# Attention heads of the second block in pairs on halves of the TensorE array, in place of one head after another

## The reference, cut to what matters

```
mixer_a: for three groups (window, dilation) = (128, 1), (512, 4), (2048, 16):
           q, k, v of 16 heads each, rotary embedding on q and k,
           causal banded attention with that dilation
         the groups are merged by their softmax denominators: one softmax
         over the three groups' scores together, o = sum of p v
         out = (o * silu(z)) @ w_out
mixer_b: q of 16 heads, k and v of 2 heads, window 128, a sink logit per head
         (it enters the maximum and the denominator, not the values)
         out = (o * silu(z)) @ w_out
```

## Time and the profile before

| what | value |
|---|---|
| median of three runs | 1861.43 us (1854.94 to 1861.74) |
| profiled execution, its own time | 1855.55 us |
| its span in the profile | 1853.3 us |
| PE busy | 1648.4 us, 89% of the span |
| DVE busy, ACT busy | 1062.3 us (57%), 929.2 us (50%) |
| mean granted TensorE clock | 0.922 |
| DMA, mean | 122 GB/s |

### The profile page before, as it was taken

The page is one execution under the profiler, slowest core; times in us unless marked ns, Lnnn a source line. Parts: engine busy times, 40 slices in busy tenths (PEclk is TensorE's granted clock), DMA queues, the critical chain, the costliest instruction groups (busy, mean ns, idle before and its releaser), DMA issues.

```text
span 1853.3 us, 26621 instructions
## 1 busy us (share of the span) xinstructions
PE 1648.4 (89%) x10291; PEld 1388.9 (75%) x10291; DVE 1062.3 (57%) x1967; ACT 929.2 (50%) x1668; POOL 105.4 (6%) x114
## 2 busy tenths in 40 slices
PE   6899888869999999779997699989999999798787
PEld 3577566637888888547665599989899998797676
DVE  1563546675343434575636776678566674576655
ACT  4353545434232313245545455558677785477635
POOL 3100023020000000020012100000000000000000
PEclk8799978888999999889987899999999999998889
DMA  8422445302323333212455256555442432342221
GB/s 291 136 68 69 159 159 180 112 28 85 120 91 92 97 107 97 70 49 67 130 161 186 91 162 201 187 178 181 144 159 92 160 121 85 114 137 76 84 69 69
DMA packets 221567, 225.45 MB, mean 122 GB/s; under 512 B 6155, under 2 KB 219985, under 8 KB 221393
## 3 DMA queue, kind: packets, MB, share of 16 engines
q1 hardware_dynamic: 220736, 223.63, 37.6%
q0 software_dynamic: 704, 0.12, 0.0%
HBM read 222.68 MB, written 1.05 MB: 121 GB/s over the span
## 4 chain that ended last, share of the span: by engine, by line
PE 71%; ACT 12%; DVE 11%; issue 3%; DMA 2%; POOL 0%; SPq 0%; DVEq 0%; ACTq 0%; POOLq 0%
PE bank L795 18%; PE bank L796 17%; PE bank L797 17%; ACT whi L1245 2%; ACT AP L1599 2%; PE bank L820 1%; ACT SH L1360 1%; PE bank L1023 1%; DVE XT L1999 1%; PE bank L866 1%; PE bank L864 1%; PE bank L865 1%; DMA raw<-in_w_mod_dram 1%; DVE AP L2221 1%; DVE wlo L1729 1%
## 5 line engine op out<-in xcount | busy, mean ns | idle before, releaser
L1729 DVE TENSOR_TENSOR wlo<-raw,whi 128x1024 fp32r<-128x1024 f32 (+3 forms) x322 | 389.5, 1210 | 326.6 <-ACT whi L1245 322.7
L1245 ACT ACTIVATE whi<-raw 128x1024 fp32r<-128x1024 f32 (+3 forms) x322 | 337.3, 1047 | 361.4 <-PE bank L797 329.1
L795 PE MATMUL bank<-HH,whi 128*128 128x512 f32 (+3 forms) x656 | 254.5, 388 | 34.6 <-DVE HL L1751 29.5
L796 PE MATMUL bank<-HL,whi 128*128 128x512 f32 (+3 forms) x656 | 250.5, 382 | 0.0
L797 PE MATMUL bank<-HH,wlo 128*128 128x512 f32 (+3 forms) x656 | 250.3, 382 | 0.0
L795 PE MATMUL bank<-HA,whi 128*128 128x256 f32 x576 | 166.8, 290 | 14.8 <-DVE LA L1751 7.4
L795 PEld LDWEIGHTS bank<-HH,whi 128*128 128x128 f32 (+2 forms) x656 | 123.3, 188 | 68.9 <-issue 23.6
L796 PE MATMUL bank<-LA,whi 128*128 128x256 f32 x576 | 163.7, 284 | 0.0
L797 PE MATMUL bank<-HA,wlo 128*128 128x256 f32 x576 | 163.6, 284 | 0.0
L797 PEld LDWEIGHTS bank<-HH,wlo 128*128 128x128 f32 (+2 forms) x656 | 123.7, 188 | 26.8 <-issue 1.0
L796 PEld LDWEIGHTS bank<-HL,whi 128*128 128x128 f32 (+2 forms) x656 | 123.9, 189 | 25.5 <-issue 1.5
(11 more groups left out here) (342 smaller groups left out, 3494.0 us busy)
## 6 DMA issues: line engine op xcount, KB each, us to landing
raw<-in_w_ff_dram SPq DMA_DIRECT2D x64, 1024.0 KB, 5.3
raw<-in_w_mod_dram SPq DMA_DIRECT2D x48, 1024.0 KB, 5.2
raw<-in_a_w_in_dram SPq DMA_DIRECT2D x40, 1024.0 KB, 5.0
raw<-in_w_in_dram SPq DMA_DIRECT2D x16, 1024.0 KB, 5.2
raw<-in_b_w_in_dram SPq DMA_DIRECT2D x9, 1024.0 KB, 5.2
raw<-in_w_out_dram SPq DMA_DIRECT2D x8, 1024.0 KB, 5.1
raw<-in_ple_w_gate_dram SPq DMA_DIRECT2D x8, 1024.0 KB, 5.2
raw<-in_a_w_out_dram SPq DMA_DIRECT2D x4, 1024.0 KB, 5.1
```

What stands on the lines that cost most here:

```text
L795: nc.tensor.matmul(o, wh, xh, start=start, stop=False)
L796: nc.tensor.matmul(o, wh, xl, start=False, stop=False)
L1245: f(whi[h % HALF_SLOTS][:, 0:n], raw[u.id % RAW_SLOTS][:, (h % 2) * n:(h % 2) * n + n], ACT.Copy)\
L1729: v.tensor_tensor(wlo[h % HALF_SLOTS][:, 0:n], raw[u.id % RAW_SLOTS][:, (h % 2) * n:(h % 2) * n + n], whi[h % HALF_SLOTS][:, 0:n].bitcast( ...
```

## The change

Heads 2p and 2p+1 become a pair p and go through four steps of their own kind instead of a third of a common step:

- `att2_first`: scores of the first 128 queries of both heads, matmuls alternating between the row halves, to banks 3 and 6; their maxima (DVE) and exponentials (ACT).
- `att2_second`: scores of the second 128 queries of both, to banks 4-5 and 6-7 (in mixer B to the rest of banks 3 and 6); their maxima and exponentials. The scaling of the probabilities, `att2_scale`, is put on DVE's late list.
- `att2_turn`: DVE runs its late list; PE transposes both heads' probabilities to banks 3, 4, 6, 7 and 5; ACT copies them to `APT`, which now holds both heads.
- `att2_pv`: values of both heads with stationary blocks of 64 columns, alternating between the column halves of bank 5; one product with the gate for all 128 rows; the high part at once on ACT, the low part on DVE's late list.

In mixer A the steps stand before units given by number (ten a group): pair 0 at 10, 11, 13, 14, pair 1 at 14, 15, 17, 18 and so on. In mixer B one `b_step` behind each unit holds the values of pair p-2, the turn of p-1 and both score steps of p; the last ones lie in the last gate unit, behind it and in the first output unit.

```diff
-    (SH0, ..., A0), o = region(o, ... ("YA1", [P, 2, SEQ]), ("APT", [P, 1152])])
+    APT = at("APT", [P, 2, 1152], where["at"])
...
+    for p, at_units in enumerate(((10, 11, 13, 14), (14, 15, 17, 18), (20, 21, 23, 24), (24, 25, 27, 28),
+                                  (30, 31, 32, 33), (33, 34, 35, 36), (36, 37, 38, 40), (39, 40, 41, 42))):
+        for kind, n in zip(("att2_first", "att2_second", "att2_turn", "att2_pv"), at_units):
+            a_slots.setdefault(n, []).append((kind, (0, p)))
+    def a_step(n):
+        for kind in ("att2_pv", "att2_turn", "att2_first", "att2_second"):
+            for st in a_slots.get(n, []):
+                if st[0] == kind:
+                    steps.append(st)
+    def a_tail():
+        a_step(41)
+        a_step(42)
+    def b_step():
+        p = b_turn[0]
+        b_turn[0] += 1
+        if p >= 2:
+            steps.append(("att2_pv", (1, p - 2)))
+        if 1 <= p <= PAIRS:
+            steps.append(("att2_turn", (1, p - 1)))
+        if p < PAIRS:
+            steps.append(("att2_first", (1, p)))
+            steps.append(("att2_second", (1, p)))
...
                 for n, (col, kind, g) in enumerate(us):
+                    a_step(10 * hq + n)
                     fm(aw, 0, col, 256, two, kind, (i, hq, g), x, seq2)
-                    if hq > 0 and n < 4 or hq == 3 and n >= 7:
-                        att2_step()
-            att2_step()
-            att2_step()
+            a_step(40)
...
                 fm(src, 0, 256 * hq + (D + 256 if kind == "az" else 0), 256, two, kind, (i, hq, 0), x, seq2,
-                   att2_step if n >= 1 else None)
-                if n >= 1:
-                    att2_step()
-            att2_step()
-            att2_step()
-            att2_step()
+                   b_step if n == 7 else None)
+                b_step()
...
             for g in range(G):
...
+                for e in (0, 1):
+                    r = slice(64 * e, 64 * e + 64)
+                    k_ = AK[buf][r, g, blk, :] if i == 0 else AK[0][r, 0, p // 4, :]
+                    ins = nc.tensor.matmul(dst[e][:, g * n:(g + 1) * n], q[r, g, blk, part * P:part * P + P], k_[:, 0:n],
+                                           start=True, stop=True)
...
             for g in range(G):
-                nc.tensor.matmul(b[:, 0:SEQ], v(g, 0), APT[:, g * SEQ:(g + 1) * SEQ], start=g == 0, stop=False)
+                for e in (0, 1):
+                    nc.tensor.matmul(b[64 * e:64 * e + 64, 0:SEQ], v(g, 0, e), att_pt(ip, e)[:, g * SEQ:(g + 1) * SEQ], start=g == 0, stop=False)
...
+        def att2_exp(ip, part):
+            act.wait_ge(s_mx2, s_mx2.at((ip, "neg", part)))
+            for e in (0, 1):
...
+                f(p_[:, a:a + n], p_[:, a:a + n], ACT.Exp, bias=small[:, neg:neg + 1], scale=SCALE,
+                  accum_out=small[:, total:total + 1]).then_inc(*s_e2.tick((ip, part, e)))
...
+        def att2_max(ip, part):
...
+            if part == 1:
+                late.append(lambda: att2_scale(ip))
+        def att2_scale(ip):
+            dve.wait_ge(s_e2, s_e2.at((ip, 1, 1)))
...
+            chain(v.reciprocal(small[:, inv:inv + 4], small[:, total:total + 4]))
+            for e in (0, 1):
+                p_ = att_p(ip, e)
+                for part, (a, n) in enumerate(((0, G * P), (G * P, G * SEQ))):
+                    c = att_col(ip, 3, e, part)
+                    ins = v.tensor_scalar(p_[:, a:a + n], p_[:, a:a + n], small[:, c:c + 1], None, ALU.mult)
+            ins.then_inc(*s_p2.tick(ip))
+        def att2_y(ip):
...
+            v.tensor_tensor(YA[buf][:, blk, :], banks[5][:, 0:SEQ], AZ[buf][:, blk, :], ALU.mult).then_inc(*s_ya.tick(ip))
+            def low():
...
+            late.append(low)
```

## The result

The changed kernel took 1885.7 us (median of 4 runs, 1878.7 to 1895.3) where the kernel before took 1858.2 beside it (4 runs): a ratio of 1.015, 95% interval 1.011 to 1.020. A second set of runs gave 1883.1 against 1862.4, ratio 1.010 (1.007 to 1.014). It is slower by 1.0 to 1.5%: 1873 was forecast, and 1848 to 1888 as its range. The forecast had +12 us over the kernel before; the two sets have +27 and +21.

What follows compares the result with a forecast made beforehand. PE was taken to bound the first mixer (A), the DVE-ACT hand-over the second (B). A +4.0, B -8.7 and clock +17 summed to +12 us: 1868 profiled, 1873 against the median, range 1848 to 1888.

Steps and rivals of the forecast that it cites:

- The halves overlap: PE in both mixers: alternating matmuls on array halves overlap fully, a pair taking 6.45 us where two heads took 10.36.
- Rival 3: PE: the halves don't overlap, PE work plus 3.9 us a pair, +10 on the forecast, 1883; chance 0.1.
- A's waits: First mixer of the second block: eight PE waits of 3.5 to 6.7 us, at banks and turns.
- The chain of 9.9 us: DVE and ACT in mixer A: from a pair's second maximum through exponentials, splits and scalings to the cosine product, 9.9 us.
- A in all: First mixer: groups two and three +4.1 us each, fourth group and tail -4.2, in all +4.0.
- the clock: Mixer A: half-speed clock after eight PE waits costs 2.1 us each, 17 in all, bounds 13.6 and 27.
- B: Second mixer: 26.4 us for two units, end 27.7, in all -8.7 us, gained by three unhidden end steps becoming one.
- B's dips stay beside it: 0: Second mixer: its chain runs on DVE and ACT, so low-clock stretches of PE cost 0.
- The sum: Whole kernel: +4.0 - 8.7 + 17 = +12 us, 1868 for the profiled execution, 1873 against the median.
- (1): Mixer A: the waits come but the clock costs little, -5 us, about 1857; chance 0.2.
- (2): Mixer A: PE stays the bound, waits under 1 us, about 1814; chance 0.15 together with half-sized waits, 1835.
- these averages hide the alternation: Mixer A: argument that DVE and ACT busy only 52 and 57 of 77.7 us doesn't rule out long PE waits.

Runs made afterwards that it cites:

- scale_now: The changed kernel with DVE scaling a pair's probabilities at once instead of behind its next weight split; 1856.2 us, ratio 0.998 to the kernel before.
- warm: The changed kernel with PE multiplying into a free bank, results unread, in seven of mixer A's waits; 1862.7 us, ratio 1.003 to the kernel before.
- after_again: The changed kernel measured once more with nothing altered; 1883.1 us (7 runs).
- spread: Changed kernel: A's exponentials and scalings behind a unit, three turns one unit later, B's at once, last low parts not late-listed; 1819.8 us, ratio 0.979.

## Why the prediction came out right, step by step

**The halves overlap** and PE saves 3.9 us a pair: shown. Values 2.10, scores 0.87 and 1.50 and eighteen transposes 1.9 are 6.4 where the forecast had 6.45. Some 1.1 of it came from putting two heads' scores in one step, 2.8 from the alternation. Rival 3 is out.

**A's waits.** Forecast 6.7 and 5.7 in each of two groups; measured 6.97, 6.53, 6.52 and 6.50. At the turns 6.5, 5.5, 4.2, 3.5 against 6.22, 5.92, 4.45 and 3.40. The chain of 9.9 us, which had the cosine product in it, measured 10.3. The second pair of a group was forecast too short by 0.8. The step's place, the instruction that ends each wait and its queue are as forecast, and scale_now showed that they react to one split by its length.

**A in all.** From the first unit of group two to the output unit that waits for the last pair:

```profile
1311.08 0.28 PE L795 MATMUL bank<-HA,whi 128*128 128x256 f32 x1
```

```profile
1324.55 0.39 PE L824 MATMUL bank<-HA,whi 128*128 128x256 f32 x1
...
1617.43 0.58 PE L824 MATMUL bank<-YH,whi 128*128 128x256 f32 x1 [2.75 <-DVE YL L1803]
```

Before it is 1580.94 less 1311.08, 269.9 us, after 292.9: +23.0. The forecast's ledger also counts the first scores of pair 0, which stand ahead of that unit (0.9): so +23.9, where it (+4.0) and the clock (+17) said +21. The waits were set right to 2 us in total, and the clock's 2.1 a wait measured 1.9 to 2.3 in warm.

**B.** Forecast -8.7, measured -4.7 from its first unit to the last low part (122.5 us before, 117.8 after). From the first to the fourth query's rope it took 80.2 us where the forecast had 78.6: two units take 26.6 in the later cycles (forecast 26.4), 26.9 in the first (25.8). Before, the same stretch took 78.2, so B's middle became longer, not "a little shorter". The end, 27.7 in the forecast, took 30.3 where it had taken 36.9: the first output unit still waited 3.06 us behind the last pair for the low part, as the timeline of PE has it:

```profile
1811.44 0.39 PE L824 MATMUL bank<-HA,whi 128*128 128x256 f32 x1 [3.06 <-DVE LA L1803]
```

This is the term of the sum that was mis-sized most, by 4 us; which instruction of the end took the extra 2.6 was not taken apart. The forecast did count the split ahead of the scaling. What it did not ask is what that split costs: scaling at once (scale_now) makes B 10 us shorter than it is after the change.

**Not foreseen.** Behind B the rest of the kernel was 3.4 us longer in the first trace. Windows of that stretch, before, after and in after_again:

```profile
1778.88:1853.30 74.42, 58.05 (x440) 55.08 (x440) 43.42 (x78) 38.08 (x67) 0.00 (x0) 0.94 0.26 86
```

```profile
1811.44:1889.30 77.86, 62.39 (x437) 60.07 (x437) 42.04 (x76) 36.19 (x65) 0.00 (x0) 0.85 0.24 82
```

```profile
1808.68:1884.50 75.82, 59.07 (x437) 56.37 (x437) 41.96 (x76) 36.11 (x65) 0.00 (x0) 0.93 0.25 84
```

At 0.50 the clock was for 10 us before, 23 after and 10 in after_again, so 2.0 of the 3.4 us differ between two executions of the same kernel and go with the clock. "B's dips stay beside it: 0" is borne out in so far as B had 37.5 us at the low clock in both the first trace and the one before.

**The sum.** +23.9, -4.7 and +3.4 is +23, 11 over the forecast's +12. The two sets measured +27 and +21 by their medians. The profiled execution shows +36; of that, 12.4 arose before the second block began (below), and none of the change's own code runs there. All three terms missed to the same side, so the measured time lies near the upper end of the range; no errors cancelled.

**The rivals.** (1) The clock costs little: out, 13 to 16 us came back in A when PE was kept at work and nothing else was changed. (2) PE stays the bound, 1814: false for this kernel. spread, a few queue positions away, has nearly that number, 1819.8, but not by that way: A is 25 us shorter than before the change where the rival had 38, and B 19 where it had 9. The argument against it, "these averages hide the alternation", was right about the change; the averages (ACT 57 and DVE 52 us of a group) were right about what was possible. In the change the evacuating engines decided: 3.6 us less PE and 8.4 more in the group. In spread ACT and DVE were as busy as in the change and the group was 6.4 us shorter than before the change. The Trainium skill's TensorEngine Tiling (Array Packing), PSUM Bottleneck, says that tiling speeds up TensorE but not the evacuation of PSUM. These two traces agree in that the evacuation limited the change, by its order and not by its amount of work.

## What to carry to other kernels

When work on one engine gets shorter, make the ledger again for the chain that releases its buffers: here a 10.3 us chain through two in-order queues began when only 3.8 us of PE's work were left ahead of the bank, and the totals (52 to 57 busy of 78 us) did not show it. Before rejecting the idea, move the slow chain behind the work that frees the bank; in spread that, with a unit more before three turns and scaling at once in B, turned +1.0 to +1.5% into -2.1% with no change in the work. Price a wait of TensorE at more than its length: here about 2 us more for each wait of 4 to 7 us that had dense work behind it.

## What the runs showed of the hardware

Keeping PE fed in a wait brought back what the clock had cost: with fillers in seven waits the granted clock stayed at 1.00 (2.4 GHz) for 269 us of A, and the banks came free no earlier.

Two heads' fp32 matmuls on different halves of the array overlap when they alternate in PE's queue: values 2.10 us a pair where full-width products took 4.02, scores 2.37 where one head behind the other took 3.22.

Identical code took different times from one execution to the next. The second block began at 1252.3 us before and at 1264.7 in the profiled execution after, at 1252.4 in spread and 1264.9 in scale_now, with the same instructions ahead of it. after_again, the same kernel as after, began it at 1255.7. Two things differ. One is the pace of 256-column matmuls in the second feed-forward, here in the groups of the pages of after, after_again and spread (busy, mean ns of one):

```profile
L824 PE MATMUL bank<-HX,whi 128*128 128x256 f32 x320 | 93.0, 291 | 9.9 <-DVE HXL L1803 5.9
```

```profile
L824 PE MATMUL bank<-HX,whi 128*128 128x256 f32 x320 | 91.8, 287 | 9.9 <-DVE HXL L1803 5.9
```

```profile
L824 PE MATMUL bank<-HX,whi 128*128 128x256 f32 x320 | 91.1, 285 | 10.0 <-DVE HXL L1817 5.9
```

The three lines of this form are 4.9 us busier in after than in spread, and the three that read FX (281 ns against 276, 256 of each) 3.6: 8.5 us. The other is the clock: 241 us of the first block were at 1.2 GHz in after and scale_now, 221 in before and spread. But after_again had 241 us too and began only 3.4 us later than before did. So the low clock goes with some 3 us of the 12 and the slower pace with most of the rest. What makes the pace slower in some executions stays open; one profiled execution against another is no measure of a per cent, and stretches are to be compared from a common start, as was done above.
